# The chunk's spreads of head maxima and weights on TensorE: contraction over 128 partitions, zeros on all but four, in place of four

## The reference, cut to what matters

```python
def _mlstm_chunk(carry, inp):
    C, n, m = carry
    q, k, v, li, lf = inp
    b = jnp.cumsum(lf, axis=-1)
    d_log = b[..., :, None] - b[..., None, :] + li[..., None, :]
    d_log = jnp.where(causal, d_log, -jnp.inf)
    inter = b + m[..., None]
    m_t = jnp.maximum(inter, jnp.max(d_log, axis=-1))
    w_intra = jnp.exp(d_log - m_t[..., None])
    w_inter = jnp.exp(inter - m_t)
    s = jnp.einsum('bhtd,bhsd->bhts', q, k) * w_intra
    num = jnp.einsum('bhts,bhsv->bhtv', s, v) + w_inter[..., None] * jnp.einsum('bhtd,bhdv->bhtv', q, C)
    den = jnp.sum(s, axis=-1) + w_inter * jnp.einsum('bhtd,bhd->bht', q, n)
    h = num / jnp.maximum(jnp.abs(den), jnp.exp(-m_t))[..., None]
```

## Time and profile before

| | |
|---|---|
| median of 3 runs | 2090.11 us (2089.05 to 2090.77) |
| the profiled execution, its time | 2090.61 us |
| its span in the trace | 2088.7 us |
| granted TensorE clock, mean over the span | 0.984 of full speed |
| PE busy | 2031.0 us, 97% of the span |
| DVE busy | 906.2 us, 43% |
| ACT busy | 498.3 us, 24% |
| POOL busy | 85.4 us, 4% |

### The profile page before, as it was taken

How to read it: one execution, slowest core, us unless ns; L and a number is a source line. 1 busy time by engine, 2 the same in 40 slices (tenths; PEclk the granted TensorE clock), 3 DMA queues, 4 the chain that set the end, 5 groups by cost and what they waited for, 6 DMA issues and landing times.

```text
span 2088.7 us, 31199 instructions
## 1 busy us (share of the span) xinstructions
PE 2031.0 (97%) x12601; PEld 2005.7 (96%) x12601; DVE 906.2 (43%) x1559; ACT 498.3 (24%) x890; POOL 85.4 (4%) x139
## 2 busy tenths in 40 slices
PE   7999999999999998999999889999999999999998
PEld 6999999999999998999999789999999999999998
DVE  6523432343234347412666755643243334333334
ACT  5202111111111124332333421412111111121122
POOL 2000000000000022000000011100000000000001
PEclk9999999999999999999999989999999999999999
DMA  6011101110011011311011340111011101110102
GB/s 205 21 41 60 60 22 39 60 60 29 31 60 60 21 56 40 82 48 29 25 31 30 104 96 21 41 61 58 18 45 60 60 20 40 60 60 20 50 1 83
DMA packets 144177, 105.10 MB, mean 50 GB/s; under 512 B 6376, under 2 KB 136248, under 8 KB 144120
## 3 DMA queue, kind: packets, MB, share of 16 engines
q1 hardware_dynamic: 143992, 104.26, 16.3%
q10 hardware_dynamic: 128, 0.03, 0.0%
HBM read 95.36 MB, written 8.92 MB: 50 GB/s over the span
## 4 chain that ended last, share of the span: by engine, by line
PE 91%; DVE 5%; ACT 1%; DMA 1%; issue 1%; SPq 1%; ACTq 0%; DVEq 0%; POOL 0%
PE bank L204 29%; PE bank L210 28%; PE bank L209 28%; PE bank L208 1%; PE bank L206 1%; DVE ffn_normed L171 1%; DVE in_lo L163 1%; PE bank L1930 1%; DMA raw<-in_w_out 1%; PE bank L1936 1%; DVE ffn_root_work L143 0%; PE bank L645 0%; PE bank L1950 0%; PE bank L1949 0%; PE bank L1923 0%
## 5 line engine op out<-in xcount | busy, mean ns | idle before, releaser
L204 PE MATMUL bank<-in_hi,w_hi 128*128 128x352 f32 x2256 | 742.2, 329 | 16.0 <-DVE in_lo L1136 7.5
L210 PE MATMUL bank<-in_hi,w_lo 128*128 128x352 f32 x2256 | 731.5, 324 | 0.0
L209 PE MATMUL bank<-in_lo,w_hi 128*128 128x352 f32 x2256 | 730.0, 324 | 0.0
L204 PEld LDWEIGHTS bank<-in_hi,w_hi 128*128 128x128 f32 x2256 | 428.6, 190 | 20.7 <-DVE in_lo L1136 8.1
L209 PEld LDWEIGHTS bank<-in_lo,w_hi 128*128 128x128 f32 x2256 | 430.7, 191 | 1.1
L210 PEld LDWEIGHTS bank<-in_hi,w_lo 128*128 128x128 f32 x2256 | 428.7, 190 | 0.0
L394 DVE TENSOR_TENSOR ffn_hidden<-ffn_silu,bank 128x352 f32<-128x352 f32 x132 | 68.8, 521 | 669.6 <-PE bank L210 579.7
L204 PE MATMUL bank<-ffn_hidden_hi,ffn_w_hi_more 128*128 128x352 f32 x1056 | 342.0, 324 | 1.2 <-ACT ffn_hidden_hi L341 1.1
L405 DVE SCALAR_TENSOR_TENSOR x<-bank,x 128x352 f32<-128x352 f32 x528 | 267.2, 524 | 159.5 <-PE bank L210 111.2
L210 PE MATMUL bank<-ffn_hidden_hi,ffn_w_lo_more 128*128 128x352 f32 x924 | 297.7, 322 | 0.0
L209 PE MATMUL bank<-ffn_hidden_lo,ffn_w_hi_more 128*128 128x352 f32 x924 | 297.4, 322 | 0.0
(11 more groups left out here) (220 smaller groups left out, 1518.2 us busy)
## 6 DMA issues: line engine op xcount, KB each, us to landing
raw<-in_ffn_w_gate SPq DMA_DIRECT2D x44, 512.0 KB, 4.0
ffn_raw_more<-in_ffn_w_down SPq DMA_DIRECT2D x44, 512.0 KB, 5.3
raw<-in_w_in SPq DMA_DIRECT2D x24, 512.0 KB, 3.8
raw<-in_ffn_w_up SPq DMA_DIRECT2D x22, 512.0 KB, 5.0
ffn_raw_more<-in_ffn_w_up SPq DMA_DIRECT2D x22, 512.0 KB, 5.3
x_parked<-x SPq DMA_DIRECT2D x3, 1408.0 KB, 5.6
x<-x_parked SPq DMA_DIRECT2D x3, 1408.0 KB, 10.9
raw<-in_w_out SPq DMA_DIRECT2D x8, 512.0 KB, 3.8
```

The costliest lines, as they stand in the source:

```text
L204: pe.matmul(out, w_hi, in_hi, start=first, stop=False)
L209: pe.matmul(out, w_hi, in_lo, start=False, stop=False)
L210: return pe.matmul(out, w_lo, in_hi, start=False, stop=last)
```

## The change

`head_row`, `pair_rows`, `row_max` and `row_inter` get 128 partitions. The computation on the four partitions stays what it is, on the first four of them; the others are zero, so the matmuls of L1923 and L1930 contract over 128 partitions and give the same numbers. POOL's clearing and filling of the two constant tensors now covers 128 partitions, and two clearings are added for `row_max` and `row_inter`, with the counts that wait for them raised by two. The matmul on `decay_row` (L1906) stays at four.

```diff
-    sh.head_row = sb("head_row", [HEADS, HEADS, P], FP32)
-    sh.pair_rows = sb("pair_rows", [HEADS, PAIRS, P], FP32)
+    sh.head_row = sb("head_row", [P, HEADS, P], FP32)
+    sh.pair_rows = sb("pair_rows", [P, PAIRS, P], FP32)
...
-        row_max = sb("row_max", [HEADS, TOKENS])
-        row_inter = sb("row_inter", [HEADS, TOKENS])
+        row_max_padded = sb("row_max", [P, TOKENS])
+        row_inter_padded = sb("row_inter", [P, TOKENS])
+        row_max, row_inter = row_max_padded[0:HEADS, :], row_inter_padded[0:HEADS, :]
...
             for n, part in enumerate((values[:, :, DV:DV + 1], state_p[:, :, :], rows[0:HEADS, ROW_KEEP, :],
-                                      rows[0:HEADS, ROW_ENM, :], max_before[:, 1:2], staged_q[:, :, :])):
+                                      rows[0:HEADS, ROW_ENM, :], max_before[:, 1:2], staged_q[:, :, :],
+                                      row_max_padded[:, :], row_inter_padded[:, :])):
                 pool.memset(part, 1.0 if n in (0, 2) else 0.0).then_inc(s.constants, 1)
-            pool.wait_ge(s.constants, 6)
+            pool.wait_ge(s.constants, 8)
...
-            dve.wait_ge(s.constants, 7)
+            dve.wait_ge(s.constants, 9)
...
-                last = pe.matmul(score_bank[:, p * GROUPS:(p + 1) * GROUPS], sh.pair_rows[:, p, :], decay_row[:, :],
+                last = pe.matmul(score_bank[:, p * GROUPS:(p + 1) * GROUPS], sh.pair_rows[0:HEADS, p, :], decay_row[:, :],
                                  start=True, stop=True)
...
-            pe.wait_ge(s.constants, 7)
+            pe.wait_ge(s.constants, 9)
...
-                    last = pe.matmul(k_bank[:, at:at + n], sh.pair_rows[:, p, :], row_inter[:, bass.ds(t0, n)],
+                    last = pe.matmul(k_bank[:, at:at + n], sh.pair_rows[:, p, :], row_inter_padded[:, bass.ds(t0, n)],
                                      start=True, stop=True)
...
-                    pe.matmul(out, sh.head_row[:, h, 0:n], row_max[:, bass.ds(t0, n)], start=True, stop=False)
+                    pe.matmul(out, sh.head_row[:, h, 0:n], row_max_padded[:, bass.ds(t0, n)], start=True, stop=False)
                     last = pe.matmul(out, sh.ident16[0:n, 0:n], sh.mask[0:n, 0:n], start=False, stop=True)
```

## The result

| | before | changed |
|---|---|---|
| median | 2089.58 us (2087.48 to 2090.77, 4 runs) | 2070.95 us (2068.24 to 2073.11, 4 runs) |
| the profiled execution | 2090.61 us | 2068.24 us |
| its span | 2088.7 us | 2066.2 us |
| mean granted clock of the span | 0.984 | 0.991 |

The ratio is 0.9911 with a 95% interval of 0.9894 to 0.9928. The change takes 18.6 us off.

The account below looks back on a forecast made before the run. The prediction took PE, busy for 97% of the span, to bound the kernel. From 2090.6 us, -9.4 (spreads) + 1.0 (group 0) - 10.9 (clock) = 2071.3, given as 2071.0 against the median; range 2066.0 to 2082.5 us.

Parts of the forecast that it names:

- rival A: Whole kernel: the forecast itself, steps close up and the chunks' clock falls go, 2071.0 us, about 2067 to 2077; chance 0.64.
- The spreads: `stage_a`, L1920 to the scores: 2.97 us becomes 1.79, saving 1.18 us a chunk and 9.4 us over eight.
- opposite step: `stage_a`, from the bf16 mask to the fp32 scores at 128 partitions: claimed to cost nothing.
- The bound that stood beside the term: `stage_a` heads, fp32 to bf16 at 128 partitions: from nothing to 0.1 us a head, 3.2 us for 32 heads.
- the passage between heights: `stage_a`: the loss read as going from four partitions to 128 and back, not as the type.
- The clock: Around six of eight chunks: half-clock falls vanish, all 10.9 us comes back; bounds nothing to 10.9.
- Group 0: `stage_a` of group 0, mask staying at 32 partitions: added alternation costs +1.0 us; bounds nothing to +1.2.
- Its clock: Around group 0: the clock fall stays, since the engine also waits there; -3 us if it goes as well.
- Cover: POOL's two added clearings, about 1.1 us each, end near 835.7, hidden by 8.5 us before DVE's scan.
- Rival B: `stage_a` chunks: steps close up but the clock still falls, only 8.4 us come, 2082 us; chance 0.24.
- Rival C: L1930 to L1931: steps come from types and the clock follows, nothing happens, 2090 plus or minus 2 us; chance 0.07.
- Rival D: Spread matmuls: 128-partition loads don't hide, +9 us in all and the clock falls stay, 2100 us; chance 0.05.

Follow-up runs that it names:

- e4: Kernel before, spreads at four partitions, with the mask's matmul over its first 32 partitions instead of 128: 2072.81 us, ratio 0.9916.
- e5: Changed kernel, spreads at 128 partitions, with the mask's matmul over its first 32 partitions: 2078.55 us, ratio 0.9947.
- e8: Kernel before, spreads at four partitions, with the four mask matmuls put together to one of 512 columns ahead of the heads: 2075.03 us, ratio 0.9927.
- e6: Changed kernel with both spreads over 64 partitions instead of 128, the mask at 128: 2079.05 us, ratio 0.9946.
- e2: Changed kernel with the maxima's spread (eight matmuls on row_max) back at four partitions, the weights at 128: 2088.04 us, ratio 0.9989.
- e3: Changed kernel with both spreads over 32 partitions instead of 128, the mask at 128: 2086.73 us, ratio 0.9991.
- e7: Changed kernel with the mask's matmul over 128 partitions in group 0 too: 2071.1 us; the changed kernel again beside it 2070.92 us.

## Why the prediction was right, point by point

- **The forecast**, 2071.0 us, against a median of 2070.95: right, rival A. The terms are less exact than the sum (which, less the 0.5 us, is 2070.8 and was given as 2071.0). That they meet to 0.1 us is luck: the spreads gave 1.2 us less than forecast and group 0 cost 0.6 us less, which half cancels, and the median of the kernel before alone moved between 2089.2 and 2089.9 us from set to set.
- **The spreads** were put at -9.4 us and came to -8.2 in the traces (1.03 us a chunk in place of 1.18), 7.6 between two medians that differ by little else. The term that was mis-sized is a change of type, but not the one that the prediction left open. From fp32 to bf16 costs nothing extra: L1932's second matmul to its mask takes 0.11 us. The "opposite step", from bf16 back to fp32, was taken at nothing on the word of the earlier trace rows, where the first score matmul starts 0.07 us behind the mask's; the cost stands one step later. The first fp32 matmul behind a mask steps at 0.165 us and not at 0.112, in three heads of a chunk, 0.05 each, which is the 0.15 us between 1.79 and 1.94. It was in the kernel before too: its eight scores take 0.165, six times 0.112 and 0.03 to the product, which makes the mean of 0.108 that the prediction took for the dense step. The bound that stood beside the term (3.2 us) held; the step behind a mask came to 0.056 us in place of 0.07.
- **That the loss is the passage between heights**, and not type or few rows, was inferred from group 0 and from the load behind the last mask. e4 and e5 show it from both sides: low with low is fast, and the gap is the same with either one low.
- **The clock** was put at -10.9 us for all six falls. All eight chunks of the changed kernel kept it in both traces, and e5 gives about -9.8 between medians. Part of the difference may be that many runs of the kernel before had a mean clock of 0.986 where the profiled one had 0.984. The reason I gave was too coarse. The steps of the alternating run are 0.11 to 0.21 us, and not "0.2 us apart and more". I wrote that gaps and few rows "point one way" and didn't say which it was; each alone keeps the clock (few rows with the gaps gone in e4 or fewer in e8, the gaps with more rows in e5 and e6), and only together was it lost (the kernel before, e2, e3). e6 and e8 show it with the whole mask in place. The forecast needed no more than that, since the padding takes both away.
- **Group 0** was put at +1.0; the traces give, from L1920 or L1922 to the scores, 1.58 us before and 1.96 and 2.00 after: +0.4. The term had the right sign and more than twice the size., on which it leans, stand at half clock (it fell at 938.9), which I didn't say: at full clock a head takes 0.09 us there (e3, e7) and 0.29 with the alternation, at half clock 0.16 and 0.38. So a head loses 0.2 us at either clock, not the chunk's 0.29, and the weights save 0.19 in place of 0.12. At equal clock that is about 4 x 0.2 - 0.19 = +0.6, an estimate; e3, with the heights of before and nearly all of the stretch at full clock, has 1.38 us there against the 1.96.
- **Its clock**, which I left in, fell for 3.4 us in both traces of the changed kernel, where it was 6.8 before; in the nine other traces it fell for 6.8 to 10.3 us. No part of the change is shown to do that.
- **Cover.** POOL's two clearings took 0.97 us each, 1.1 had been estimated, and the last ended at 835.4, 8.8 us ahead of the scan (`mix_values` is still cleared first, at 830.72; the list of rows above lacks it):

```profile
833.34 0.97 POOL L1349 MEMSET mix_row_max<- 128x1056 f32 x1
...
835.29 0.10 POOL L1352 MEMSET mix_rows<- 4x9 f32 x1
```

PE's waits for DVE and ACT in the chunks stayed at 1.9 and 2.5 us, as argued: both chains start at PE.
- **Rival B** (steps close, clock falls) didn't come. (Its 16 turning and spreading matmuls are 18: 4, 2, 4 and 8.) Its mirror, steps open and clock kept, did, in e5 and e6, at 2079. **Rival C** is refuted by e4. **Rival D**, with the rule of the Trainium skill (TensorE: Matmul & The Clock Gate, What overlaps and what doesn't) that loads slide under running matmuls only where the row group differs: the trace speaks against it at 128 partitions on 128, where the mask's load starts 0.11 us ahead of its matmul while L1932 runs. The Trainium skill's other rule, that a change of the tiling mode drains the engine (TensorEngine Tiling, Key Properties), fits all of it: in e3 and e6 32 and 64 rows beside 128 cost what four do, and in e4 four beside 32 cost nothing. That a drain is what happens inside is not shown by any run; what is shown is the gap.

## What to carry to other kernels

Where a small matmul contracts over a few partitions and stands between full-height ones, read the starts, not the lengths: here each return trip between heights cost 0.24 us a head (0.575 against 0.333). Either bring both to one height (the zeros took no time in the matmuls here, and their clearing was covered) or put the low ones together so that the heights meet once. Check the granted clock around such a run: here it was worth more (about 9.8 us) than the gaps themselves (7.6 to 8.2), and much of it was lost on the products that follow.

## What the runs showed of the hardware that I had not expected

The clock. With the same gaps (2.96 to 2.98 us from the turns to the scores; 2.86 in e5), spreads of four or 32 partitions came with a mean clock of 0.981 to 0.987 in every run, and spreads of 64 or 128 with 0.989 to 0.990; with the gaps gone or fewer (e4, e8), four partitions had 0.989 to 0.990 as well. No run of the one group reached into the other. The closest pair is e3 and e6: from 32 to 64 partitions, all but four of them zero in both, the steps stay (2.97 and 2.98 us) and the falls go from four of the eight chunks to none. So the number of partitions, zeros with them, made a difference to the clock here that it didn't make to the steps. In the traces the clock over the chunks is 0.94 (before, e2) and 0.96 (e3) in the one group and 1.00 (e4, e5, e6) in the other. Why it is lost only with both was not tried further.
